# A two-part block on one core: mixers of the second part reordered, and the modulation ahead of the gathers moved off ScalarE

## The chip, the cores and the metric

One core of a Trainium2 chip runs the whole kernel. The metric is the device time of one execution in microseconds. The core has five engines with a queue each, worked off in order: TensorE (PE, matrix products into PSUM, and transposes), VectorE (DVE), ScalarE (ACT), GpSimd (POOL, which also issues the gathers) and SyncE (SP, which issues the weight loads). They wait for each other on semaphores only.

## The reference

One sequence of 256 tokens, width 1024, goes through two parts.

- First part: six modulation vectors `mod = silu(c) @ w_ada + b_ada` (each 1024 wide); an RMS norm with shift and scale; a projection; eight heads of forgetting attention and eight of stick-breaking attention, each head's output normed and all of them projected by `w_out`; then a second modulated norm and a layer that picks, for each token, 16 experts in each of 8 heads (128 rows of 2 x 1024 values per token, gathered from memory), takes 128 dot products, a gelu and a gated sum.
- Second part, two layers. Layer 0: a projection `x @ w_in`, rotary embedding, four heads of differential attention (two softmax maps a head, subtracted) with a norm, and four heads of plain causal attention ("moba", which is that at 256 tokens), both projected by `w_out`; a layer norm; a squared-relu feed-forward of width 4096; a layer norm. Layer 1: gated linear attention (GLA) with decays, a norm and a silu gate, then the same two norms and a feed-forward.

```python
mod = c_act @ w_ada[l] + b_ada[l]
a = diff_attention(dq, dk, dv, lam, subln, lambda_init)
b = moba_attention(mq, mk, mv)
return jnp.concatenate([merge_heads(a), merge_heads(b)], axis=-1) @ w_out
x = layer_norm(DEEPNORM_ALPHA * x + mix, ln_mix_g[l], ln_mix_b[l])
```

## The kernel before

**Weights.** Every weight matrix is cut in tiles of 1024 x 512 (2 MB). A tile is loaded whole in one of four buffers `W`; `load_on` (L347) issues the loads in the planned order, each once the tile before it in its buffer is done. A dense tile is then split in two parts of less precision, so that a product takes three matrix products: four pieces of `split_piece` (L359), each one ScalarE copy to `WH` (three buffers) and one subtraction to `WL` on VectorE. The splits do not stand where they are needed. They wait in a list `behind`; `tick(n)` (L366) takes up to n entries off its head while they may run (tile's load issued, the former tile in its `WH` buffer done), and `take` (L378) emits what is left of a tile just before its use. `fm_tile` (L524) runs a tile with features as rows (four half groups of 24 products with 256 columns, two to a PSUM bank); `tm_tile` (L539) runs it with tokens as rows (two groups of 24 products with 512 columns). Both call `tick` and a hook between groups, and the hook is how other work gets between dense products on TensorE's queue.

**Ahead of the gathers.** The modulation tiles 4 to 9 are made by `ada_rows` (L684). Of a tile's eight rows blocks VectorE multiplies and adds 0 to 3, ScalarE scales 4 to 7 (`some`, L692), and GpSimd adds up ScalarE's four results and VectorE's sum in four additions (`sums`, L706); both steps of a tile stand in `behind`. `close` (L715) is one product with ones on TensorE, which adds over the partitions. It ends the tile, so that the next load in its buffer starts. `stick_breaking` (L973) gives one step per hook: a score product, three ScalarE operations, two of VectorE and two of GpSimd for head i, a product and as many operations again for head i-1, and the values for head i-2. Order of the list: L811 to 816 and L983 to 1009.

**Gathers.** `gather` (L1352) issues 256 gathers from GpSimd, each 128 rows of 8 KB; VectorE takes the dot product, TensorE adds up. The last query tile (`queries`, L1297) is computed between the first four.

**Second part, layer 0.** After two V tiles come four projection tiles with rotary embedding (L1553 to 1556). `evac_rope` (L1526) copies a bank on ScalarE, has TensorE multiply the copy by a rotation matrix at once, and finishes on VectorE. Then `attention` (L822) runs twice as a generator, differential and moba attention in turn: each step emits the scores of head i (`scores`: per map one product pair, one VectorE pass, two maxima, two ScalarE exponentials), then the weights and transposes of head i-1 (`weights`, `turned`), then the values of head i-2. The norm of the differential output, the scaling of moba's and their transposes follow. `close_pair` (L551) runs the output projection and the layer norm.

**Layer 1.** `ffn` (L1648) ends in a layer norm whose second half of tokens is transposed at once (`give`, L477, `last`, L485). GLA: the narrow gate projection, q, the gate sums, k, two silu tiles, two V tiles; each group of these four calls the next step of `levels` (L1756: GpSimd makes decays, VectorE operands and results, TensorE products, eight levels). Then the head products, a norm per half of the tokens, the transposes, and `close_mixer` (L1689).

Of the kernel before, what the change touches and what calls it, by code (L numbers as in the profile page):

```python
# [182 lines left out]
def build(nc, A, out, C1, C2):  # L183
    ctx = ExitStack()
    with ctx:
# [48 lines left out]

        def bank():
            b = turn[0] % 4
            turn[0] += 1
            return b
# [53 lines left out]
        w_ada(9, 3)  # L292
        wout.append(wplan(A["w_out"], 0, 0, 0, 0))
        wq.append(wplan(A["w_query"], 0, 0, 2, 2))
        wout.append(wplan(A["w_out"], 0, 512, 3, 1))
# [6 lines left out]
        for j, s, h in ((2, 2, 0), (5, 1, 1), (0, 0, 2), (1, 3, 0), (3, 2, 1), (4, 1, 2)):  # L302
            hyt.append(wplan(A["hy_w_in_2"], 0, j * 512, s, h))
        later_w, later_h = itertools.cycle((0, 3, 2, 1)), itertools.cycle((0, 1, 2))
# [18 lines left out]
        gla_in = {j: wplan_on(A["gla_w_in_2"], 0, j) for j in (0, 1, 4, 5, 2, 3)}  # L323
# [200 lines left out]
        def fm_tile(tile, evac, *tokens, xtok=None, hook=None, n=2):  # L524

            take(tile)
            for c in range(0, 4, 2):
                b = bank()
                for j in range(2):
                    w = slice((c + j) * 128, (c + j + 1) * 128)  # L530
                    tk = dense(PS[b][:, j * 256:(j + 1) * 256], tile, fm_pairs(tile, w), *tokens, *bank_free[b], xtok=xtok)
                    if j == 1:
                        bank_free[b] = evac(b, c, tk)
                    tick(n)
                    if hook:
                        hook()
            wdone(tile, tk)

        def tm_tile(tile, evac, *tokens, hook=None, n=4):  # L539

            take(tile)
            for t in range(2):
                b = bank()
                tk = dense(PS[b][:, :], tile, tm_pairs(tile, t), *tokens, *bank_free[b], mid=hook)
                bank_free[b] = evac(b, t, tk)
                tick(n)
# [3 lines left out]

        def close_pair(pair, norm, *tokens, n=2):  # L551

            for t in range(2):
                for j in range(2):
                    b = bank()
                    take(pair[j])
                    tk = dense(PS[b][:, :], pair[j], tm_pairs(pair[j], t), *tokens, *bank_free[b], mid=norm.mid if (j, t) == (1, 1) else None)
                    if t == 1:
                        wdone(pair[j], tk)
                    norm.give(j, b, t, tk)  # L560
                    if (j, t) != (1, 1):
                        tick(n)
# [121 lines left out]
        def ada_rows(j, direct=()):  # L684
# [5 lines left out]
            t = {}  # L690

            def some(ks, kp):  # L692
                def step():
                    if ks[0] == 0:
                        accumulate(acc, tile, ks, *acc_free[half])
                    else:
                        for k in ks:
                            dve(lambda e: e.scalar_tensor_tensor(out=acc, in0=tile.w[:, k, :], scalar=silu_c[:, k:k + 1], in1=acc,
                                                                 op0=ALU.mult, op1=ALU.add))
                    t["d"] = dve.last  # L700
                    for k in kp:
                        t["a"] = act(lambda e: e.activation(tile.w[:, k, :], tile.w[:, k, :], ACT.Copy, scale=silu_c[:, k:k + 1]),
                                     t_cb, tile.arrived, ordered=False)
                return step

            def sums():  # L706
                w = tile.w
                pool(lambda e: e.tensor_tensor(w[:, 4, :], w[:, 4, :], w[:, 5, :], ALU.add), t["a"])
                if not direct:
                    pool(lambda e: e.tensor_tensor(w[:, 6, :], w[:, 6, :], w[:, 7, :], ALU.add))  # L710
                    pool(lambda e: e.tensor_tensor(w[:, 4, :], w[:, 4, :], w[:, 6, :], ALU.add))
                t["p"] = pool(lambda e: e.tensor_tensor(w[:, 4, :], w[:, 4, :], acc, ALU.add), t["d"])
                acc_free[half] = (t["p"],)

            def close():  # L715
                b = bank()
                tk = mm(PS[b][:, :], [(silu_c[:, k:k + 1].broadcast_to([128, 128]), tile.w[:, k, :]) for k in direct] +
                        [(ones, tile.w[:, 4, :])], t["p"], *bank_free[b])
# [8 lines left out]
            a, b = some((0, 1), (4, 5)), some((2, 3), () if direct else (6, 7))  # L727
            return [(cond, a), (cond, lambda: (b(), sums()))], (cond, close)
# [82 lines left out]
        later_split(win[1])  # L811
        t_zs = zero_q(QS, t_turned)
# [3 lines left out]
        later_ada(4)  # L816
# [156 lines left out]
        def stick_breaking():  # L973
            for i in range(10):
# [4 lines left out]
                if 0 <= i - 2 < 8:  # L979
# [3 lines left out]
        later_close(4)  # L983
# [4 lines left out]
        tm_tile(win[2], evac_tok(lambda t: V[:, t, 512:1024]), hook=lambda: hooks.pop(0)())  # L988
        t_vs = (act.last, dve.last)
        later_ada(5)  # L990
        later_ada(6)
        later_close(5)
# [5 lines left out]
        later_close(7)  # L998
# [5 lines left out]
                        values_in=lambda: t_vf)  # L1004
        later_ada(8)
        later_ada(9)
        later_close(8)
        later_close(9)
        later_split(wout[0])
# [4 lines left out]
        tm_tile(win[5], evac_tok(lambda t: V[:, t, 0:512]), hook=lambda: hooks.pop(0)(), n=5)  # L1014
# [3 lines left out]
        def norm_half(i, write):  # L1018
# [944 lines left out]
```

How the kernel before makes its waits and increments, by code:

```python
    def wait(self, *tokens):  # L100
        for sem, value in tokens:
            if value > self.seen.get(sem.name, 0):
                self.seen[sem.name] = value
                self.steps.append(lambda e, s=sem, v=value: e.wait_ge(s, v))
# [1 line left out]
    def __call__(self, make, *tokens, ordered=True):  # L106
        self.wait(*tokens)
        if ordered:
            self.wait(self.last)
        self.n += 1
        self.steps.append(lambda e, m=make(LATER), s=self.sem: m(e).then_inc(s, 1))
        return self.last
# [4 lines left out]
    def dma(self, make, slot, *tokens):  # L118
        self.wait(*tokens)
        slot.n += 16
        self.steps.append(lambda e, m=make(LATER), s=slot.sem: m(e).then_inc(s, 16))
        return (slot.sem, slot.n)
```

## Time and profile before

| | us |
|---|---|
| median of 3 runs | 1717.49 |
| lowest and highest run | 1708.98, 1719.38 |
| the profiled execution: whole time | 1713.44 |
| its span in the trace | 1711.6 |
| busy: TensorE, VectorE, ScalarE, GpSimd | 1380.6, 1131.3, 539.2, 454.7 |

Times in the trace are us from the start of the span. A row of a timeline or of the waits names what released the idle time before it; a line number can be that of a helper that records every operation, so the tile names say what the operation is: `W` a raw weight tile, `WH` and `WL` its split, `LNV<-W` the modulation's products, `EB<-PS` stick-breaking and the mixers' scores, `XH` and `XL` the split and transposed activations.

### The profile page before, as it was taken

How to read it: one execution, taken by the hardware profiler on the slowest of the kernel's cores; microseconds unless marked ns; L12 is line 12 of the kernel's file. 1: busy time of each engine (PE TensorE's matmuls, PEld its weight loads, DVE VectorE, ACT ScalarE, POOL GpSimd, SP SyncE). 2: the span in 40 equal slices, each digit the busy share in tenths (PEclk: the TensorE clock that was granted, in tenths of full speed). 3: DMA queues.
4: the chain of work that ended last, by engine and by line, in shares of the span. 5: the costliest groups of instructions: out<-in, count | busy, mean ns of one | idle time of the engine just before them, and what ended most of it. 6: DMA issues, size and time to landing. Idle time of an engine off the chain costs nothing.

```text
span 1711.6 us, 17345 instructions
## 1 busy us (share of the span) xinstructions
PE 1380.6 (81%) x6264; PEld 971.9 (57%) x6264; DVE 1131.3 (66%) x2051; ACT 539.2 (32%) x1023; POOL 454.7 (27%) x393
## 2 busy tenths in 40 slices
PE   6976788777777677777777788658999899789998
PEld 5875668523223232222222267547999687679996
DVE  6655665688887788886555556647756659577564
ACT  2453434222221213212111233323434246234341
POOL 1154305244443443544444200000211025001110
PEclk9988899999998999999999989878999999889999
DMA  9554526799999999999999823204555534245550
GB/s 367 190 184 148 196 74 227 293 421 409 421 421 412 421 408 382 400 422 420 422 421 421 344 75 123 98 25 142 182 196 197 189 110 147 75 151 179 188 197 25
DMA packets 116629, 433.17 MB, mean 253 GB/s; under 512 B 6832, under 2 KB 7088, under 8 KB 83520
## 3 DMA queue, kind: packets, MB, share of 16 engines
q0 software_dynamic: 36864, 268.45, 38.0%
q1 hardware_dynamic: 79392, 162.51, 26.8%
q8 instruction: 50, 0.82, 0.2%
q10 hardware_dynamic: 288, 1.11, 0.2%
q14 instruction: 35, 0.29, 0.0%
HBM read 431.00 MB, written 1.05 MB: 252 GB/s over the span
## 4 chain that ended last, share of the span: by engine, by line
PE 47%; DMA 23%; DVE 19%; ACT 6%; issue 2%; POOL 2%; SPq 0%; DVEq 0%; ACTq 0%; POOLq 0%
PE PS L45 45%; DMA EB<-in_experts,EI 22%; DVE EB L78 5%; DVE WL L75 3%; ACT BIG L24 2%; PE PS L84 1%; DVE X L63 1%; POOL W L75 1%; ACT WH L24 1%; DVE Y L75 1%; DMA W<-in_w_ada 1%; DVE GV L75 1%; DVE EB L63 1%; DVE XL L75 1%; DVE ST L69 1%
## 5 line engine op out<-in xcount | busy, mean ns | idle before, releaser
L45 PE MATMUL PS<-EB,BIG 128*128 128x512 f32 x1024 | 495.4, 628 | 169.9 <-ACT BIG L24 169.8
L45 PEld LDWEIGHTS PS<-EB,BIG 128*128 128x128 f32 x1024 | 190.3, 197 | 470.3 <-ACT BIG L24 287.3
L78 DVE CUSTOM_DVE_ANT_0 EB<-EB,Y 128x1024 f32<-128x1024 f32 x256 | 313.4, 1224 | 146.0 <-DMA EB<-in_experts,EI 145.0
L39 POOL DMA_INDIRECT EB<-in_experts,EI x256 | 288.3, 1126 | 397.0 <-PE PS L45 380.9
L75 DVE TENSOR_TENSOR WL<-W,WH 128x1024 fp32r<-128x1024 f32 x228 | 297.5, 1351 | 109.5 <-ACT WH L24 109.3
L45 PE MATMUL PS<-XH,WH 128*128 128x256 f32 x928 | 272.0, 293 | 12.8 <-DVE WL L75 10.0
L24 ACT ACTIVATE WH<-W 128x1024 fp32r<-128x1024 f32 x240 | 237.8, 1047 | 91.8 <-PE PS L45 84.9
L45 PE MATMUL PS<-XL,WH 128*128 128x256 f32 x928 | 265.0, 286 | 0.0
L45 PE MATMUL PS<-XH,WL 128*128 128x256 f32 x928 | 265.0, 286 | 0.0
L45 PEld LDWEIGHTS PS<-XH,WH 128*128 128x128 f32 x928 | 180.9, 195 | 17.9 <-DVE WL L75 11.1
L45 PEld LDWEIGHTS PS<-XL,WH 128*128 128x128 f32 x928 | 180.8, 195 | 2.7 <-issue 2.4
L45 PEld LDWEIGHTS PS<-XH,WL 128*128 128x128 f32 x928 | 180.6, 195 | 0.0
L24 ACT ACTIVATE BIG<-BIG 128x2 f32<-128x2 f32 (+1 forms) x136 | 31.1, 228 | 442.5 <-DVE BIG L78 442.0
L75 POOL TENSOR_TENSOR AL<-Y,AH 128x512 fp32r<-128x512 f32 x32 | 41.5, 1298 | 459.9 <-DVE AH L66 459.9
L24 ACT ACTIVATE BIG<-K,BIG 128x128 f32<-128x128 f32 x256 | 100.3, 393 | 58.8 <-DVE BIG L75 57.9
L45 PE MATMUL PS<-WH,XH 128*128 128x512 f32 x240 | 102.8, 428 | 10.8 <-DVE XL L75 6.4
L45 PE MATMUL PS<-WL,AH 128*128 128x512 f32 x256 | 101.3, 396 | 0.0
L45 PE MATMUL PS<-WH,AH 128*128 128x512 f32 x256 | 100.8, 394 | 0.0
L45 PE MATMUL PS<-WH,AL 128*128 128x512 f32 x256 | 100.3, 392 | 0.0
L45 PE MATMUL PS<-WL,XH 128*128 128x512 f32 x240 | 98.9, 412 | 0.0
L45 PE MATMUL PS<-WH,XL 128*128 128x512 f32 x240 | 98.7, 411 | 0.0
L24 ACT ACTIVATE Y<-Y 128x512 f32<-128x512 f32 (+1 forms) x40 | 28.7, 718 | 118.7 <-DVE Y L72 113.5
(170 smaller groups left out, 1512.1 us busy)
## 6 DMA issues: line engine op xcount, KB each, us to landing
W<-in_ffn_w SPq DMA_DIRECT2D x32, 2048.0 KB, 8.8
W<-in_w_ada SPq DMA_DIRECT2D x12, 2048.0 KB, 12.2
W<-in_w_in SPq DMA_DIRECT2D x6, 2048.0 KB, 12.9
W<-in_hy_w_in SPq DMA_DIRECT2D x6, 2048.0 KB, 13.5
W<-in_gla_w_in SPq DMA_DIRECT2D x6, 2048.0 KB, 7.9
W<-in_w_query SPq DMA_DIRECT2D x4, 2048.0 KB, 8.2
W<-in_w_out SPq DMA_DIRECT2D x2, 2048.0 KB, 8.3
EB<-in_experts,EI POOLq DMA_INDIRECT x256, 11.1
```

Source lines behind the costliest of these rows:

```text
L24: return lambda e: e.activation(*a, **k)
L39: return lambda e: e.indirect_dma_start(*a, **k)
L45: return lambda e: e.matmul(*a, **k)
L63: return lambda e: e.scalar_tensor_tensor(*a, **k)
L69: return lambda e: e.tensor_reduce(*a, **k)
L75: return lambda e: e.tensor_tensor(*a, **k)
L78: return lambda e: e.tensor_tensor_reduce(*a, **k)
L84: return lambda e: e.transpose(*a, **k)
```

## The change

Ahead of the gathers:
- `ada_rows` uses VectorE and GpSimd alone. VectorE takes row blocks 0 to 4, GpSimd multiplies 5, 6 and 7, and adds them and VectorE's sum: three steps in the list (products 0, 1 and GpSimd's 5; products 2, 3 and GpSimd's 6 with an addition; product 4 and GpSimd's 7 with two additions).
- The order in the list: tile 4's steps stand ahead of the first projection tile, tile 5's ahead of the third, each close one place earlier, and the split of `wout[0]` ahead of the last close. `tm_tile` gets ticks in the middle of a group (`inside`). `w_out`'s first tile is loaded ahead of modulation tile 9, in another buffer.
- `drain()` before the last query tile.

In the second part:
- `evac_rope` leaves the rotation for later; `behind_group`, the hook of the four tiles, runs it after the next half group. From the tenth of the 16 half groups on it also takes one step of the differential attention, so that its six steps stand among the last two tiles. Moba follows alone, with the norm of the differential output (`norm_half`) spread over its steps. The `WH` buffers of tile 6 of the projection and of the tiles behind it change, so that the mixers' buffers are free.
- The output projection first sums rows 0 to 511 (the differential half) of all four groups, with moba's scaling and transposes behind the first group, then rows 512 to 1023.
- `ffn(0)` leaves the transposes of its second half of tokens until two V groups of the GLA have run on the first half; the V tiles now stand ahead of the gate, q and k, and `levels` goes on in the middle of a group too, among the two silu tiles alone.
- The GLA's second half is normed before the output projection's first half runs, and transposed behind that.
- `bank()` no longer hands out a bank that is being filled.

```diff
-            a, b = some((0, 1), (4, 5)), some((2, 3), () if direct else (6, 7))
-            return [(cond, a), (cond, lambda: (b(), sums()))], (cond, close)
+            def products(ks):
+                for k in ks:
+                    if k == 0:
+                        accumulate(acc, tile, (0,), *acc_free[half])
+                    else:
+                        t["d"] = dve(lambda e: e.scalar_tensor_tensor(out=acc, in0=w[:, k, :], scalar=silu_c[:, k:k + 1], in1=acc,
+                                                                      op0=ALU.mult, op1=ALU.add))
+            def beside(k):
+                pool(lambda e: e.tensor_scalar(w[:, k, :], w[:, k, :], silu_c[:, k:k + 1], None, ALU.mult), t_cb, tile.arrived)
+                if k > 5:
+                    pool(lambda e: e.tensor_tensor(w[:, 5, :], w[:, 5, :], w[:, k, :], ALU.add))
+                if k == 7:
+                    t["p"] = pool(lambda e: e.tensor_tensor(w[:, 5, :], w[:, 5, :], acc, ALU.add), t["d"])
...
+            steps = [(cond, lambda ks=ks, k=k: (products(ks), beside(k))) for ks, k in (((0, 1), 5), ((2, 3), 6), ((4,), 7))]
...
         later_split(win[1])
+        later_ada(4)
...
-        later_close(4)
+        later_ada(5)
         later_split(win[3])
...
-        later_ada(5)
+        later_close(5)
         later_ada(6)
-        later_close(5)
         later_split(win[4])
...
+        def behind_group():
+            fresh[0] += 1
+            if fresh[0] % 2:
+                rotate_one()
+            if fresh[0] == 10:
+                mixing.append(attention(4, lambda i: QD[:, i, :], lambda i: KD[:, i // 2, :],
...
+                                        maps=2, lam=lam, tokens=(act.last, dve.last, *hyt[2].done), done=diff_done))
+            if fresh[0] >= 10:
+                next(mixing[0], None)
...
+        for _ in moba:
+            for _ in range(2):
+                if steps:
+                    steps.popleft()()
+            tick(2)
...
+                dense(PS[b][:, :], hy_out[j], tm_pairs(hy_out[j], t), diff_x["x", t], *bank_free[b], ks=range(4), stop=False)
+                if (j, t) == (0, 0):
+                    write_moba(0)
+                    write_moba(1)
+                else:
+                    tick(2)
...
+        ffn(0, t_xt, norm, beside=lambda free: wg_parts.append(narrow_parts(wg, 16, 0, t_wg, *free)), turn=False)
+        first_v = []
+        for j in range(2):
+            b = bank()
+            take(gla_in[2 + j])
+            first_v.append((b, dense(PS[b][:, :], gla_in[2 + j], tm_pairs(gla_in[2 + j], 0), norm.xt[0], *bank_free[b])))
+        norm.last()
...
         for j in range(2):
-            tm_tile(gla_in[4 + j], with_levels(evac_silu(j)), n=2)
-        for j in range(2):
-            tm_tile(gla_in[2 + j], with_levels(evac_tok(lambda t: VG[:, t, j * 512:(j + 1) * 512])), n=2)
+            tm_tile(gla_in[4 + j], with_levels(evac_silu(j)), hook=lambda: next(lv, None), n=2)
...
+        t_head_x = turn_tile(Y[:, 0, :], 0, gla_norm(0))
+        ready = gla_norm(1)
```

## Rows read from the trace of the kernel before

**Rows 1.** The chain that ended last, the page's shares by engine.

```profile
PE 47%; DMA 23%; DVE 19%; ACT 6%; issue 2%; POOL 2%; SPq 0%; DVEq 0%; ACTq 0%; POOLq 0%
```

**Rows 2.** Windows: stretch, length, PE, PEld, DVE, ACT, POOL busy, clock, DMA share, GB/s.

```profile
60.00:155.00 95.00, 79.01 (x492) 71.11 (x490) 53.86 (x67) 44.90 (x73) 42.59 (x50) 0.89 0.44 155
320.00:976.00 656.00, 485.87 (x1020) 187.94 (x1019) 476.76 (x1142) 140.46 (x414) 280.60 (x249) 0.97 1.01 415
1088.00:1129.00 41.00, 24.63 (x110) 21.55 (x111) 25.28 (x69) 13.67 (x52) 0.00 (x0) 0.72 0.08 32
1129.00:1147.00 18.00, 6.13 (x29) 4.50 (x28) 7.70 (x14) 6.42 (x12) 0.00 (x0) 0.59 0.00 0
1147.00:1182.00 35.00, 27.15 (x113) 21.55 (x113) 22.91 (x39) 8.76 (x15) 0.00 (x0) 0.84 0.43 150
1363.00:1399.00 36.00, 28.05 (x208) 26.92 (x209) 20.70 (x32) 15.90 (x21) 0.95 (x1) 0.86 0.38 128
1399.00:1470.00 71.00, 64.70 (x356) 54.38 (x355) 63.64 (x60) 33.30 (x40) 30.38 (x20) 0.99 0.42 148
1487.00:1523.00 36.00, 27.99 (x113) 22.23 (x114) 23.15 (x40) 9.40 (x16) 0.00 (x0) 0.83 0.48 162
```

**Rows 3.** Groups by form ahead of the gathers: count, busy, mean ns, idle before.

```profile
L75 POOL TENSOR_TENSOR W<-W 128x512 f32<-128x512 f32 x18 | 26.3, 1463 | 25.8 <-ACT W L24 24.5
...
L24 ACT ACTIVATE W<-W,ST 128x512 f32<-128x512 f32 x24 | 15.3, 706 | 0.0
```

**Rows 4.** Timeline of ScalarE: start, us, operation, idle before; stick-breaking, last evacuation.

```profile
90.18 0.49 ACT L24 ACTIVATE EB<-PS 128x384 f32<-128x384 f32 x1
...
96.73 0.49 ACT L24 ACTIVATE EB<-PS 128x384 f32<-128x384 f32 x1
...
154.03 0.60 ACT L24 ACTIVATE BIG<-PS 128x512 f32<-128x512 f32 x1 [5.96 <-PE PS L45]
```

**Rows 5.** Timeline of TensorE ahead of the gathers, two of its waits.

```profile
103.70 2.07 PE L45 MATMUL PS<-EB,K 128*128 128x256 f32 x6 [3.66 <-ACT W L24]
...
171.52 1.22 PE L45 MATMUL PS<-W,K 128*128 128x512 f32 x1 [8.85 <-POOL W L75]
```

**Rows 6.** Timeline of VectorE: one product alone, one beside GpSimd's additions.

```profile
131.49 0.75 DVE L63 SCALAR_TENSOR_TENSOR LNV<-W,ST,LNV 128x512 f32<-128x512 f32 x1
...
168.72 1.63 DVE L63 SCALAR_TENSOR_TENSOR LNV<-W,ST,LNV 128x512 f32<-128x512 f32 x1
```

**Rows 7.** Timeline, rotary projections: three rotation products, one VectorE operation behind them.

```profile
1031.15 2.08 PE L45 MATMUL PS<-BIG,GV 128*128 128x512 f32 x2 [3.23 <-ACT BIG L24]
...
1040.27 1.12 PE L45 MATMUL PS<-BIG,GV 128*128 128x512 f32 x2 [0.69 <-ACT BIG L24]
...
1047.68 1.13 PE L45 MATMUL PS<-BIG,GV 128*128 128x512 f32 x2 [0.69 <-ACT BIG L24]
...
1048.84 0.69 DVE L75 TENSOR_TENSOR Y<-PS,GV 128x512 f32<-128x512 f32 x1 [2.16 <-PE PS L45]
```

**Rows 8.** Timeline of VectorE in a mixer step: first score, first and last weights.

```profile
1102.86 0.56 DVE L63 SCALAR_TENSOR_TENSOR EB<-PS,K 128x384 f32<-128x384 f32 x1
...
1105.76 0.18 DVE L60 RECIPROCAL ST<-ST 128x4 f32<-128x4 f32 x1
...
1107.27 0.48 DVE L63 SCALAR_TENSOR_TENSOR EB<-EB,ST 128x256 f32<-128x256 f32 x1
```

**Rows 9.** Timeline of TensorE: waits behind the feed-forward's norm and the GLA's norm.

```profile
1369.54 1.97 PE L84 MATMUL PS<-K,X 128*128 128x128 f32 x8 [6.58 <-DVE X L63]
...
1483.60 2.15 PE L84 MATMUL PS<-K,Y 128*128 128x128 f32 x8 [5.03 <-DVE Y L63]
```

**Rows 10.** Groups by form: split halves at 60 to 245, and in the levels.

```profile
L75 DVE TENSOR_TENSOR WL<-W,WH 128x1024 fp32r<-128x1024 f32 x24 | 28.8, 1238 | 18.7 <-ACT WH L24 18.7
...
L24 ACT ACTIVATE WH<-W 128x1024 fp32r<-128x1024 f32 x28 | 28.0, 1045 | 2.2 <-DMA W<-in_w_in 2.1 <-issue 0.2
...
L75 DVE TENSOR_TENSOR WL<-W,WH 128x1024 fp32r<-128x1024 f32 x20 | 30.5, 1569 | 0.0
```

More of the change, by code:

```diff
@@ L689, in ada_rows @@
             o = GV[:, kind - 2, half * 512:half * 512 + 512]
[L690 to L695, printed above, removed]
-                    else:
[L697 to L713, printed above, removed]
+            w, t = tile.w, {}
@@ L1296, in build @@
         later_split(wq[3])
+        drain()
         queries = query_groups(3)
@@ L1564, in build @@
                          lambda h, t: V[:, t, 512 + h * 128:512 + (h + 1) * 128], 128, 6, 128.0 ** -0.5,
-                         part(GVf[:, 2688:3840], 3), [*part(BIG[:, 5120:5888], 2), buf(9)], tokens=t_proj, base=16, done=moba_done)
-        mixers = [diff, moba]
-        while mixers:
-            for g in list(mixers):
-                if next(g, True):
-                    mixers.remove(g)
-            tick(2)
-        hs, hr, ht = (a[:, 0:8] for a in (hs_, hr_, ht_))
-        tq = []
-        for t in range(2):
-            ta = act(lambda e: e.activation(Y[:, t, 0:512], PS[4 + t][:, :], ACT.Copy), diff_done["out"])
-            tq.append(act(lambda e: e.activation(PS[4 + t][:, :], Y[:, t, 0:512], ACT.Square), ta))
@@ L1890, in build @@
                     r.append(td)
-            t_heads.append(turn_tile(Y[:, t, :], t, r))
-        t_xt = t_heads[-2:]
+            return r
+        t_head_x = turn_tile(Y[:, 0, :], 0, gla_norm(0))
+        ready = gla_norm(1)
         ln_free[0] = (dve.last, pool.last, pe.last)
-        t_xt = close_mixer(1, gla_out, t_xt)
+        norm = layer_norm(A["ln_mix_g_2"][1], A["ln_mix_b_2"][1])
+        first = []
+        for j in range(2):
+            b = bank()
+            take(gla_out[j])
+            first.append((b, dense(PS[b][:, :], gla_out[j], tm_pairs(gla_out[j], 0), t_head_x, *bank_free[b])))
+        t_head_x = turn_tile(Y[:, 1, :], 1, ready)
+        for j, (b, tk) in enumerate(first):
+            norm.give(j, b, 0, tk)
+            tick(2)
+        for j in range(2):
+            b = bank()
+            tk = dense(PS[b][:, :], gla_out[j], tm_pairs(gla_out[j], 1), t_head_x, *bank_free[b], mid=norm.mid if j else None)
+            wdone(gla_out[j], tk)
+            norm.give(j, b, 1, tk)
+            if j == 0:
+                tick(2)
+        t_xt = norm.tokens
         t_out = []
```

190 lines of the change are left out of this document (110 added, 80 removed).

## The prediction

> **What bounds the kernel now.** I read the chain of work that ended last first: TensorE has 47% of it, transfers 23%, VectorE 19% [rows 1]. No engine bounds the whole, so the windows by stage come next [rows 2]. From 320 to 976 us the transfer engines are full (share 1.01, 415 GB/s); nothing in the change touches that stage, so it only moves as a block. All that can be won lies in stretches where TensorE is idle and its clock low: ahead of the gathers (79 of 95 us busy at a granted clock of 0.89), the mixers (24.6 of 41 at 0.72) and the norm behind them (6.1 of 18 at 0.59), and the joints around the feed-forwards. The levels of the GLA are the opposite: TensorE 64.7 and VectorE 63.6 of 71 us, both nearly full. The timelines then show each wait.
>
> **Ahead of the gathers.** Removed: 24 scalings on ScalarE, 15.3 us [rows 3]. Added: one VectorE product for each of six tiles, and two GpSimd operations for each (six for four). ScalarE's queue is where they hurt: at 103.70 TensorE waited 3.66 us with ScalarE's scaling ahead of the stick-breaking's exponential [rows 5].
> The sum goes by the pace of stick-breaking. A step without a wait took 96.73 - 90.18 = 6.55 us [rows 4]. Six more heads start, 39.3 us; the two last steps start none, and I take 9.7 for both (four half groups' pace below, less the missing score); two closes on the path are 0.9 each. 90.18 + 39.3 + 9.7 + 1.8 = 141.0, against the evacuation at 154.03 [rows 4]: at best 13 us. The loads allow it, since each close stands earlier: the tile that the last projection needs is freed one tile sooner. Against it stand GpSimd's operations. The second and third step come in one tick, five operations of 1.46 us [rows 3], 7.3 us, into a gap of some 5 between the mask operations of two heads; I charge 2.5 for each of the two tiles that lie beside stick-breaking, which leaves 8. The 8.85 us wait at 171.52 is that of tile 8's close for GpSimd [rows 5]. Its sums now begin a half group sooner, but VectorE's product and the last addition still follow the group: some 5 us stay, 3.9 go. Tile 9 is now loaded behind `wout[0]`, and its close stands in the forgetting attention: +3. Sum -9.
> GpSimd's multiplication by a column has no row. Nothing excludes that it is nearly free; above, its subtraction of twice the size is the next row, and the addition at 1.46 is nearest and is what I took. At 2.4 it costs three more per tile, of which about a third on the path: +6. Nearly free it gives -3. So this part is -20 (all waits gone) to +3.
> The other cost: VectorE's product takes 0.75 us alone and 1.63 beside GpSimd's additions [rows 6]. The Trainium skill (SBUF — State Buffer, "SBUF: two separate sides") has the access that the two share as an exclusive lock, held for a whole instruction, and the trace agrees. That rule speaks against moving ScalarE's part to GpSimd, and is the second rival below. The skill's GPSIMD Engine Reference (Engine selection) puts a one-input operation near line rate; by it a multiplication would be about half of the addition, some 0.7, this part -12 and the total 1687.5 as an estimate. No row here shows it.
> `drain()` I cost at nothing: VectorE and ScalarE reach those splits behind the same score evacuations as now.
>
> **Rotation.** TensorE waits for the ScalarE copy of each pair of half groups: 3.23 once and 0.69 seven times [rows 7]. Run a half group later, the copy is done: -8.1, call it -8. The cover is that half group: 7.41 us between two rotations (1040.27, 1047.68), less 0.69 and 1.12, is 5.6, so 2.8 each.
>
> **Mixers.** A differential step holds VectorE from 1102.86 to 1107.75, 4.9 us [rows 8], and TensorE's scores, transposes and values add 1.9: 6.8. A moba step by the same operations is 3.4. The sum, 10.2, is the pace of the present loop (41 us for four [rows 2]). TensorE runs in order, and the transposes of a step wait for weights that VectorE makes behind this step's scores. So a hook stops the dense products for its whole chain: putting the differential steps between half groups hides none of the 6.8. It exposes more. At group 10 the scores wait for the newest splits (copy 0.6, two of 1.05, one of 1.24 [rows 10]): 3.9. At 11 and 13 the rotation's three passes of 0.69 [rows 7] stand ahead, 1.5 each. At 14 the weights wait behind splits, 3.2. Sum 10.1; between 4 and 10.1 I take 8, as some splits will be early. Against it, the 18 us from 1129 to 1147 [rows 2] go: the differential norm lies in moba's steps, moba's scaling behind the first output group (2.8 us of cover for about 2). But in moba VectorE, the bound, gets that work and four pieces of split: 7.7 us and 5.0, with ScalarE's 4 x 1.05 in the same chain. Between 8 and 16 I take 10. 8 + 10 - 18 = 0. The clock: five half groups of 2.8 now stand among waits of 4 to 7 us, and such a stretch has 0.72 [rows 2]: 1.1 each, 5.4; it was granted 1.00 before. Half of it, +2.5, since the two last groups stand denser. The output projection keeps its order of size: its second halves leave less time (4.2 us) for the first norm (6), which eats what the earlier scaling gives. Sum +2.5, from -8 to +12.
>
> **Feed-forward to GLA.** The wait of 6.58 us [rows 9] disappears under two V groups, 11 us, and the clock stays up (0.86 in that stretch). But 22.2 us of dense products leave the levels, where they covered VectorE. What is late next: the dense work up to the first level ends at 1363 + 54 = 1417 (V 22.2, transposes 3.3, gate projection 2.8, q and k 22.2, the rest 3.6). VectorE's list in the levels is 63.6 less twelve pieces of 1.57 [rows 10] and two evacuations of 0.7: 43.4, and TensorE's 64.7 - 22.2 = 42.5, nearly equal, in turns; 5 us of mutual waits gives 1465.5 against 1469.5 now: -4, from -9 to +3.
>
> **GLA's output.** The projection starts on the first half while the second is normed: the 5.03 us [rows 9] go and TensorE starts 7 us sooner, then waits 2.4 for the second half's split: -4.5.
>
> **Sum.** -9 - 8 + 2.5 - 4 - 4.5 = -23, against the profiled execution's 1713.4 (span 1711.6): 1690.4, I say 1690.5. The median of the runs is 1717.5, 4 us above that execution, so this is 1.6% under it.
>
> **Rivals.**
> *More is hidden than I allow.* If stick-breaking meets its pace (-16), the mixers' splits are always early and the clock holds (-6), and the levels run without mutual waits (-9): -16 - 8 - 6 - 9 - 4.5 = -43.5, 1670. For it: the pace of 6.55 was really seen. Against: it asks for luck in three places.
> *The gain is given back to the shared engines.* All 30 products run at 1.63, 48.9 us, where 24 at the mean of the two rows, 1.19, are 28.6: +20 us on VectorE, and with 0.6 of it on the path, +12, the first part is +3. With the mixers at +5.5 and the levels at 0: +3 - 8 + 5.5 + 0 - 4.5 = -4, 1709.5. For it: the slower product [rows 6], and both engines full in the levels. Against: products have slack at 131, where one ran alone.
> *Slower.* The hooks keep TensorE's granted clock at its lower level, 1.2 GHz, from the ninth half group to the end of the output projection. The 22.2 us of projection double, the projection behind them goes from 27.2 at 0.84 to some 44 (+17), the mixers' 17.7 us at full clock to 35.5 (+11): +50, 1740. It decides once the mean clock there is under 0.55. Against: even the stretch that was idle for two thirds had 0.59 [rows 2].
>
> **Chances.** Forecast case 0.50 (1675 to 1706), more hidden 0.20, given back 0.20, slower 0.08, something else 0.02. The range 1664 to 1717 reaches into both neighbours and leaves 2 in 10 out. Under 1700.3 (1% below the median, about what a measurement of this kernel can tell from no change) lie the second case and four fifths of the first: 0.61; within 1%: 0.30; slower: 0.09.
>
> **What would show it.** Stick-breaking starts 6.5 to 7 us apart and the first gather some 9 us earlier; ScalarE without `W<-W`. No 0.69 waits before rotations. Hooks of 6.8 us among the last two projection tiles at a clock near 0.75, and moba with its norm in 25 to 29 us. No wait of 6.6 ahead of the GLA, but its levels ending only 4 us sooner. I am wrong if GpSimd's multiplication is far from the addition, if VectorE's products all take 1.6, or if a hook of the mixers costs much less or more than 6.8.

## The result and the profile after

The changed kernel takes 1744.25 us (median of 4 runs, 1743.53 to 1746.07) against 1715.83 of the kernel before: ratio 1.0175, 95% interval 1.0144 to 1.0207, which lies clear of no change. It is 28 us slower where I forecast 27 us faster, and outside my range. The profiled execution has a span of 1742.4 us.

The chain of work that ended last is shared out as before [rows 1]:

```profile
PE 47%; DMA 23%; DVE 20%; ACT 5%; issue 2%; POOL 2%; SPq 0%; DVEq 0%; ACTq 0%; POOLq 0%
```

Windows by stage of the changed kernel, with the columns of [rows 2]:

```profile
60.00:155.00 95.00, 76.67 (x487) 70.03 (x486) 57.95 (x68) 34.54 (x56) 57.35 (x57) 0.89 0.43 153
...
1060.00:1122.00 62.00, 38.87 (x220) 34.49 (x220) 29.68 (x64) 14.44 (x41) 0.00 (x0) 0.81 0.12 38
1122.00:1152.00 30.00, 14.20 (x56) 11.78 (x57) 18.81 (x36) 12.17 (x29) 0.00 (x0) 0.54 0.17 63
1152.00:1191.00 39.00, 28.93 (x126) 22.48 (x124) 23.03 (x40) 8.43 (x15) 0.00 (x0) 0.89 0.41 134
1363.00:1417.00 54.00, 50.99 (x289) 43.52 (x288) 36.65 (x52) 22.82 (x31) 0.96 (x1) 1.00 0.47 164
...
1445.00:1512.00 67.00, 42.10 (x204) 36.54 (x204) 39.93 (x47) 20.64 (x34) 18.36 (x13) 0.79 0.18 63
```

Ahead of the gathers ScalarE lost 10 us of work and GpSimd gained 15, and TensorE is no busier. From 1363 to 1417 TensorE works almost without a gap at full clock, as the new V groups were meant to bring; but behind 1445 it is busy 42 of 67 us, where the levels before had 64.7 of 71 [rows 2]. There the time went.

Five marks cut every trace into the same stages: the load of `hy_w_in` that the end of the last query tile releases (ahead of the gathers); the first product of the two V groups that stand ahead of the rotary projections (13.9 us of the stage are theirs); the first product of the layer 0 output projection; the first product of the feed-forward; the load of the second layer's `ln_ffn`, counted from that of the first.

| stage, us | before | after | difference | predicted |
|---|---|---|---|---|
| ahead of the gathers | 317.6 | 317.4 | -0.1 | -9 |
| gathers, to the V groups | 690.6 | 692.0 | +1.4 | 0 |
| rotary projection and mixers | 138.5 | 142.9 | +4.4 | -5.5 |
| output projection, layer 0 | 35.1 | 39.2 | +4.1 | 0 |
| `ln_ffn` to `ln_ffn` (feed-forward, GLA, its output) | 337.2 | 356.9 | +19.7 | -8.5 |
| span | 1711.6 | 1742.4 | +30.8 | -23 |

The rest of 1.3 us lies behind the last mark. The gathers' stage is the same code in all kernels of this study and lies between 686.4 and 692.0 us in their traces, so a difference of single traces under about 3 us says nothing there; the medians carry the verdicts.

### The profile page after: what moved, and what is told of

Its sections match the earlier page's. It is cut to its first block, busy times and chain, and to the rows that moved or that the text cites. A ratio compares the mean times of both kernels' runs of the same rounds, so it can differ in the third digit from the quotient of the medians.

```text
span 1742.4 us, 17343 instructions
## 1 busy us (share of the span) xinstructions
PE 1386.0 (80%) x6264; PEld 976.7 (56%) x6264; DVE 1144.5 (66%) x2058; ACT 523.7 (30%) x998; POOL 482.2 (28%) x405
## 4 chain that ended last, share of the span: by engine, by line
PE 47%; DMA 23%; DVE 20%; ACT 5%; issue 2%; POOL 2%; SPq 0%; DVEq 0%; ACTq 0%; POOLq 0%
PE PS L45 46%; DMA EB<-in_experts,EI 22%; DVE EB L78 4%; DVE WL L75 3%; ACT BIG L24 2%; DMA W<-in_w_ada 1%; PE PS L84 1%; DVE Y L75 1%; ACT WH L24 1%; DVE X L63 1%; DVE LNV L63 1%; DVE EB L63 1%; DVE ST L69 1%; DVE XL L75 1%; DVE GV L75 1%
## 5 line engine op out<-in xcount | busy, mean ns | idle before, releaser
L75 DVE TENSOR_TENSOR WL<-W,WH 128x1024 fp32r<-128x1024 f32 x228 | 305.2, 1387 | 131.6 <-ACT WH L24 131.5
```

The lines of the kernel that those rows point to most:

```text
L75: return lambda e: e.tensor_tensor(*a, **k)
```

## The experiments

Sixteen of the seventeen kernels are built on the kernel before, with parts of the change added. Each is timed against the kernel before on its own chip (medians 1714.35 to 1715.93).

**Each part alone.** The first four (`a_alone`, `rot_alone`, `mix_alone`, `gla_alone`) leave out the norm of the GLA and the transposes behind it, and the last three of them also carry one line of the part ahead of the gathers:

```diff
-        tm_tile(win[5], ..., hook=lambda: hooks.pop(0)(), n=5)
+        tm_tile(win[5], ..., hook=lambda: hooks.pop(0)(), n=3, inside=2)
```

> The kernel before with the part ahead of the gathers alone (modulation on VectorE and GpSimd, its order and its loads). Theory 1, the ledger of the two traces: each part does alone what its stretch shows in the changed kernel, and here that is 0 us (the last query tile ends at 317.58 before and 317.44 after), so the time is within 4 us of before and the wait at about 171 is 5 us. Theory 2, the parts disturb each other (loads and splits of one against another), and alone this part brings my -9: 0.995 of before.

> The kernel before with the rotation behind the next half group and nothing else changed. Both theories have the 0.69 us waits and the one of 3.23 us gone: -8 us, ratio 0.995. If the rotation's VectorE passes run into the first scores of the mixers instead, -5.

> The kernel before with the rotation deferred, the differential steps among the last projection tiles, the norm in moba's steps and the output projection in two halves of its sum. Theory 1: +8.6 us as in its stretch of the changed kernel, ratio 1.005, with TensorE waits of 4 to 6 us in five or six hooks. Theory 2: my -5.5, ratio 0.997. With rot_alone at -8, theory 1 puts +16 to +17 on the reordering itself.

> The kernel before with the V groups of the GLA ahead of gate, q and k, the transposes of the second half behind two of them, and the levels in the middle and at the end of the four silu groups. Theory 1: +19 to +20 us, ratio 1.011, with waits of 6 to 7 us for operands in the middle of each silu group. Theory 2: my -4, ratio 0.998.

Measured: 1707.23, 1686.93, 1707.05 and 1719.71 us (ratios 0.9951, 0.9840, 0.9966, 1.0036). None can be set against the kernel before as it stands. The next batch repeats the parts with the norm in place. `rot_tick` is `rot_alone` with the norm; the rotation and the line above are its only edits to the order of work:

```diff
+                turning.append(rotate)      # rotation product and its passes
...
+        fm_tile(hyt[2], evac_rope(...), *t_xt, hook=behind_group)   # and so hyt[3], hyt[4], hyt[5]
```

> The kernel before with the rotation deferred and with the last projection tile ahead of the gathers taking two entries of the list in the middle of a group and three behind it, in place of five behind it; nothing else. This is rot_alone with the GLA's norm, which rot_alone, mix_alone, a_alone and gla_alone leave out (in gla_alone in its new form, in the others in the old one), together with the same change of the list. Theory 1: the norm is worth 10 to 11 us by the load marks of the traces, so 1697 to 1698, ratio 0.990; the wait of 8.85 at 171 has become two waits of 2 and 4. Theory 2: the gain of rot_alone was the missing norm alone, and this is 1709, ratio 0.995.

> mix_alone with the GLA's norm in place and without the change of the list ahead of the gathers. Theory 1 (ledger of the traces, +8.6 us for rotation, mixers and output projection): 1719 to 1724, ratio 1.003 to 1.005. Theory 2 (my sum, -5.5): 1709, ratio 0.997.

> The kernel before with everything from the end of the first feed-forward to the second layer's output projection as in the changed kernel, the rest as before. Theory 1: +19 for the levels and -1 for the output, 1733, ratio 1.011. Theory 2 (my sum, -8.5): 0.995.

Measured: `rot_tick` 1699.35 us, ratio 0.9924 (0.9902 to 0.9946), so the missing norm is worth 12.4 us. `mix_only` 1727.0, ratio 1.0063 (1.0042 to 1.0084), 3 us above what its first theory had. `gla_only` 1732.72, ratio 1.0108 (1.0089 to 1.0126), as its first theory had it. Corrected by 12.4, `a_alone` is at 1719.6, 5 us above before. The correction is a rough one: it puts `gla_alone` at 1732.1, level with `gla_only`, although `gla_alone` has the middle tick too. By the marks:

| stage, us | before | rot_tick | mix_only | gla_only | after |
|---|---|---|---|---|---|
| ahead of the gathers | 317.6 | 314.4 | 321.1 | 318.4 | 317.4 |
| rotary projection and mixers | 138.5 | 128.1 | 142.9 | 139.1 | 142.9 |
| output projection | 35.1 | 35.1 | 39.1 | 34.9 | 39.2 |
| `ln_ffn` to `ln_ffn` | 337.2 | 337.2 | 338.9 | 360.7 | 356.9 |

Each part costs alone what its stage shows in the changed kernel; theory 2, a disturbance between parts, falls. The first row differs between kernels with the same code there (317.6, 321.1 and 318.4: mean 319.0), so I take means: the whole part ahead of the gathers (part A), in `a_alone`, the changed kernel and `lv_first` below (322.2, 317.4, 320.6), is 320.1, +1. The one line with the middle tick, in the eight kernels that otherwise have the old list and loads (309.7 to 315.2), is 313.3, nearly 6 us less than before. No run has this line alone.

**Levels.** `lv_first` changes the order of issue at the end of a silu group and nothing else:

```diff
                 tk = dense(PS[b][:, :], tile, tm_pairs(tile, t), *tokens, *bank_free[b], mid=mid)
+                if early:
+                    hook()
                 bank_free[b] = evac(b, t, tk)
...
-                if hook:
+                if hook and not early:
                     hook()
...
-            tm_tile(gla_in[4 + j], with_levels(evac_silu(j)), hook=lambda: next(lv, None), n=2)
+            tm_tile(gla_in[4 + j], with_levels(evac_silu(j)), hook=lambda: next(lv, None), n=2, early=True)
```

> The changed kernel, where at the end of each of the four silu groups the step of the levels is issued ahead of the group's evacuation and of the pieces of split, not behind them. Theory R (the ring: the operands that the next half group waits for stand behind the silu evacuation on ScalarE, VectorE and GpSimd and behind the splits): the three waits of 6.4 to 6.8 us fall to 2 to 3, and it is 10 to 13 us faster than the changed kernel, ratio to the kernel before 1.010. Theory W (too little dense work against VectorE's and GpSimd's own work in the levels, in whatever order): within 3 us of the changed kernel, ratio 1.016 to 1.018.

Measured: 1725.91 us, ratio 1.0068 (1.0046 to 1.0090), 18 us faster than the changed kernel; its last stage is 338.9 against 356.9. Here is the ring in the changed kernel, from the timelines of TensorE, ScalarE, VectorE and GpSimd in this order:

```profile
1446.29 3.78 PE L45 MATMUL PS<-Y 128*128 128x128 f32 x16 [6.36 <-DVE Y L75]
...
1465.35 3.78 PE L45 MATMUL PS<-GV 128*128 128x128 f32 x16 [6.84 <-DVE GV L75]
...
1453.96 0.60 ACT L24 ACTIVATE BIG<-PS 128x512 f32<-128x512 f32 x1 [5.51 <-PE PS L45]
1454.59 1.29 ACT L24 ACTIVATE BIG<-BIG 128x512 f32<-128x512 f32 x2
...
1462.09 1.06 ACT L24 ACTIVATE Y<-Y 128x1024 f32<-128x1024 f32 x1 [4.30 <-POOL Y L75]
...
1455.92 0.69 DVE L75 TENSOR_TENSOR BIG<-PS,BIG 128x512 f32<-128x512 f32 x1 [7.28 <-ACT BIG L24]
1456.87 4.18 DVE L75 TENSOR_TENSOR WL<-W,WH 128x1024 fp32r<-128x1024 f32 x2 [0.26 <-ACT WH L24]
1461.15 1.56 DVE L33 COPY_PREDICATED LNV<-GV,PS 128x512 f32<-128x512 int32 x2
1462.75 2.54 DVE L75 TENSOR_TENSOR GV<-BIG,GV 128x512 f32<-128x512 f32 x2
...
1456.69 1.30 POOL L75 TENSOR_TENSOR BIG<-BIG,LNV 128x512 f32<-128x512 f32 x1 [9.33 <-DVE BIG L75]
1458.43 6.31 POOL L75 TENSOR_TENSOR Y<-BIG 128x512 f32<-128x512 f32 x4 [0.44 <-POOL BIG L75]
```

A group ends and ScalarE evacuates it at 1453.96. VectorE's silu product follows at 1455.92, then its two pieces of split. GpSimd's silu product stands at 1456.69, and only behind it, from 1458.43 on, come the decays of two steps. Their exponential on ScalarE is at 1462.09, the operands on VectorE at 1462.75, and TensorE, which had only the first half of the next group to do (2.8 us), has waited since 1458.5 for them, until 1465.35. The next evacuation needs that group's second half. The ring turns once in 18.2 and 17.6 us (1453.96, 1472.12, 1489.68) for two steps. In the kernel before the products that need the operands stand a whole group later, and their waits are 0.28 to 1.0 us. With the step ahead of the evacuation the same two products wait less, and ScalarE's evacuations follow without a wait, 12.4 and 11.9 us apart:

```profile
1448.53 2.05 PE L45 MATMUL PS<-Y 128*128 128x128 f32 x16 [2.31 <-DVE Y L75]
...
1461.97 3.78 PE L45 MATMUL PS<-Y 128*128 128x128 f32 x16 [4.01 <-DVE Y L75]
...
1438.27 0.60 ACT L24 ACTIVATE BIG<-PS 128x512 f32<-128x512 f32 x1
...
1450.67 0.60 ACT L24 ACTIVATE BIG<-PS 128x512 f32<-128x512 f32 x1
...
1462.57 0.60 ACT L24 ACTIVATE BIG<-PS 128x512 f32<-128x512 f32 x1
```

Theory R holds, and by more than the 10 to 13 us that it said; theory W falls. From the second silu group to the head products TensorE waits 28.4 us in the changed kernel (6.36, 6.84, 6.71, 7.62, 0.91), 12.5 in `lv_first` (2.31, 4.01, 6.16) and 5.6 before (0.28, 0.71, 1.00, 3.61). What is left of the part was tried on top of `rot_tick` (the edit is that of `v_one` against `gla_combo`):

> rot_tick with the GLA of the changed kernel and the step of the levels ahead of each silu evacuation, as in lv_first. The parts add: gla_only gave +17.7 and lv_first took back 18, so 1699, ratio 0.992, level with rot_tick. Against it: if the parts of a kernel disturb each other by several us, it is 1705 or 1693.

> gla_combo with one V tile ahead of the levels and the other behind the silu tiles; one step of the levels at the end of each silu group (ahead of its evacuation), two in each of the last two V groups. The wait of 6.58 us at the end of the feed-forward stays filled by the one V group. If dense work between the steps is what was missing in gla_combo, the levels run at the old pace of 7 us a step and it is 4 to 7 us faster than rot_tick: 1693 to 1695, ratio 0.988. If two steps in a V group run into the same ring, level with rot_tick, 0.992.

```diff
-        for j in range(2):
+        for j in range(1):
...
-            tm_tile(gla_in[4 + j], with_levels(evac_silu(j)), hook=lambda: next(lv, None), n=2, early=True)
+            tm_tile(gla_in[4 + j], with_levels(evac_silu(j)), hook=ends_only, n=2, early=True)
+        tm_tile(gla_in[3], with_levels(evac_tok(...)), hook=lambda: next(lv, None), n=2, early=True)
```

Measured: `gla_combo` 1699.04 us, ratio 0.9917 (0.9888 to 0.9946); `v_one` 1699.46, ratio 0.9904 (0.9868 to 0.9940). Both are level with `rot_tick`, as the sum of the parts had it for the first, and the second does not bring the 4 to 7 us of its first theory. Their last stages are 337.9 and 337.2 against 337.2. The 6.58 us of the feed-forward [rows 9] are gone in each, and come back in the levels: in `v_one` TensorE is busy 29.8 of 43 us there and VectorE 36.5:

```profile
1417.00:1460.00 43.00, 29.75 (x160) 25.80 (x159) 36.50 (x38) 17.18 (x20) 16.25 (x11) 0.88 0.29 98
```

That VectorE's own list sets the pace once dense products leave is my reading of such windows; no run takes work off VectorE there, and it stays argued.

**Mixers.** `mix_late` starts the differential attention behind the last projection group; `mix_skew` keeps it in turn with moba, two steps ahead. Both have the middle tick of `rot_tick`, and the norm in moba's steps and the output projection of the changed kernel.

```diff
-            if fresh[0] == 10:
+            if fresh[0] == 16:
+                rotate_one()
...
-            if fresh[0] >= 10:
-                next(mixing[0], None)
```

> mix_only with the change of the list of rot_tick, and with the differential steps alone behind the last projection group, none among the groups. Theory H (steps among the half groups cost more than alone, by splits, rotation passes and the slower clock of the half groups; 42 us there): 6.8 us a step, 34 to 36 in all, so 7 us faster than mix_only with that list, 1715, ratio 1.000. Theory N (the order among the groups hides something; norm and output are the loss): 1723 to 1728, ratio 1.005 to 1.007.

> rot_tick with the differential attention two steps ahead of moba, the other four in turn with it as before, the differential norm in the last two steps of moba and the output projection in two halves of its sum. If the pairing in turn is what the changed kernel gave up (a pair takes 10.2 us, the two apart 6.8 and 7 to 8), the paired part costs as before, and the 18 us stretch of the norm shrinks by 8 while the two single steps and the output's second half take back 6 to 10: 1697 to 1701, ratio 0.991 to 0.993. If it is the norm's place that costs, 1708 or more, 0.996.

Measured: `mix_late` 1703.46 us, ratio 0.9926 (0.9901 to 0.9951); `mix_skew` 1704.56, ratio 0.9942 (0.9923 to 0.9961). Of the 23.5 us between `mix_only` and `mix_late`, 14.4 lie in the stage of the mixers (142.9 against 128.5) and 5.9 ahead of the gathers. Theory H holds, and by twice what I gave it; `mix_skew` lies between its two theories. Here are TensorE's waits in the changed kernel, with the steps among half groups (the first row is the first scores, the others are the weights), then those for the weights in `mix_late`, with the steps alone:

```profile
1059.96 2.90 PE L45 MATMUL PS<-BIG 128*128 128x128 f32 x8 [4.07 <-issue]
...
1073.97 0.90 PE L84 MATMUL PS<-K,EB 128*128 128x128 f32 x3 [5.92 <-DVE EB L63]
...
1084.29 0.90 PE L84 MATMUL PS<-K,EB 128*128 128x128 f32 x3 [4.34 <-DVE EB L63]
...
1097.62 0.90 PE L84 MATMUL PS<-K,EB 128*128 128x128 f32 x3 [5.84 <-DVE EB L63]
...
1109.13 0.90 PE L84 MATMUL PS<-K,EB 128*128 128x128 f32 x3 [6.05 <-DVE EB L63]
```

```profile
1081.35 0.90 PE L84 MATMUL PS<-K,EB 128*128 128x128 f32 x3 [4.43 <-DVE EB L63]
...
1088.52 0.90 PE L84 MATMUL PS<-K,EB 128*128 128x128 f32 x3 [3.71 <-DVE EB L63]
...
1096.98 0.90 PE L84 MATMUL PS<-K,EB 128*128 128x128 f32 x3 [3.71 <-DVE EB L63]
```

In `mix_late` the projection ends at the pace of `rot_tick` (70 us) and the differential attention takes 31.6 us behind it. In the changed kernel the two together take 112.3: 42 for the attention. The stage as a whole is 128.5 in `mix_late`, 128.2 in `mix_skew` and 128.1 in `rot_tick`: neither new order wins anything over the old loop with the norm behind it. No run keeps the old loop and moves the norm alone. And both pay for the output projection in two halves: 39.2 and 41.0 us against 35.1.

**Ahead of the gathers.** Five kernels, all with the rotation deferred and the middle tick in the last projection tile, separate the list, the loads and the engines:

> rot_tick with the whole new order ahead of the gathers (list, loads, ticks in the middle of a group, drain) but the modulation as before: four scalings on ScalarE, four additions on GpSimd a tile. Theory E (the move from ScalarE to GpSimd is what costs in this part, the order is free or brings a little): 1694 to 1700, at or below rot_tick, ratio 0.989 to 0.992. Theory O (the order and the later loads of the query tiles cost): 1704 to 1708, ratio 0.995.

> rot_tick with the modulation on VectorE and GpSimd as in the changed kernel (three steps a tile), in the old order of the list and with the old loads. Theory O (order_only has shown the loss of this part to be in the order, 7.7 us, and the move of the engines to be free there): 1697 to 1702, ratio 0.991 to 0.993. Theory E' (the move costs as much as the order, and the two only do not add because both hold the same GpSimd queue): 1705 to 1709, ratio 0.995.

> order_only with the loads as before (w_out's first tile behind modulation tile 9, in its old buffer). Theory L (the loads cost: the first query tile is loaded at 197 us in order_only and at 166 in rot_tick): as rot_tick, 1699 to 1702, ratio 0.992. Theory Q (the list costs: two tiles' additions stand ahead of stick-breaking's masks on GpSimd, waits of 7.03, 4.50 and 7.56 us): as order_only, 1705 to 1708, ratio 0.995.

> rot_tick with the loads of the changed kernel (w_out's first tile ahead of modulation tile 9 and in another buffer), the list and the engines as in rot_tick. Theory S (the gain of the new loads is theirs: list_only is at 1714.5 and order_only, which differs by the loads alone, at 1707.0): 1691 to 1693, ratio 0.987. Theory P (the loads pay only where the list holds the closes back): 1698 to 1703, ratio 0.992.

> loads_only with the middle tick in the third projection tile too (two entries in the middle of a group, two behind it, in place of four behind it). If what the middle tick buys in the last tile is the earlier close and nothing else, this does nothing here: within 2 us of loads_only. If GpSimd's additions come apart in general, 3 us faster.

| kernel | list | loads | scaling | stage, us | median, us | ratio (95%) |
|---|---|---|---|---|---|---|
| rot_tick | old | old | ScalarE | 314.4 | 1699.35 | 0.9924 (0.9902 to 0.9946) |
| loads_only | old | new | ScalarE | 317.0 | 1701.75 | 0.9929 (0.9903 to 0.9954) |
| loads_tick2 | old, one more middle tick | new | ScalarE | 314.0 | 1702.59 | 0.9944 (0.9922 to 0.9965) |
| list_only | new | old | ScalarE | 329.4 | 1714.49 | 1.0000 (0.9982 to 1.0018) |
| order_only | new | new | ScalarE | 320.5 | 1707.03 | 0.9950 (0.9934 to 0.9967) |
| eng_only | old | old | GpSimd | 328.2 | 1711.56 | 0.9974 (0.9956 to 0.9991) |

The new list costs 15 us with the old loads, twice what theory Q had, and the new loads give 7 of them back but nothing by themselves (theory P). The move from ScalarE to GpSimd costs 12 us in the old order (theory E', and more than it said; `eng_only` also has three entries a tile in the list for two); in the new order it costs nothing that can be seen (320.5 against the mean of 320.1 with all of part A). The cause that theories Q and E' give, GpSimd's queue in front of stick-breaking's masks, is there. GpSimd and TensorE in `list_only`:

```profile
83.19 5.80 POOL L75 TENSOR_TENSOR W<-W 128x512 f32<-128x512 f32 x3 [15.75 <-ACT W L24]
89.14 2.06 POOL L75 TENSOR_TENSOR W<-W,LNV 128x512 f32<-128x512 f32 x1
...
94.67 2.08 PE L45 MATMUL PS<-EB,K 128*128 128x256 f32 x6 [7.15 <-POOL EB L75]
```

Tile 5's additions come 14 us sooner than in the kernel before (96.71), and the first mask of stick-breaking stands behind them. But this is not where the 15 us go:

| time in the trace, us | before | rot_tick | order_only | list_only | eng_only | after |
|---|---|---|---|---|---|---|
| last wait for a mask ends | 144.3 | 144.4 | 143.7 | 145.5 | 152.5 | 146.5 |
| last product of the last projection tile | 182.9 | 181.5 | 180.5 | 182.6 | 181.9 | 179.7 |
| first transposes behind the forgetting attention | 210.9 | 206.8 | 212.9 | 221.9 | 221.5 | 211.8 |

At the end of the last projection tile `list_only` and `eng_only` are at most 1 us behind `rot_tick`; the forgetting attention behind it takes 39.3 and 39.6 us where it took 25.3. ScalarE and then TensorE in `list_only`, and the same in `eng_only`:

```profile
208.38 1.06 ACT L24 ACTIVATE WH<-W 128x1024 fp32r<-128x1024 f32 x1 [9.98 <-DMA W<-in_w_out]
...
210.36 0.90 PE L84 MATMUL PS<-K,EB 128*128 128x128 f32 x3 [4.74 <-ACT EB L24]
...
191.14 1.06 ACT L24 ACTIVATE WH<-W 128x1024 fp32r<-128x1024 f32 x1 [7.17 <-DMA W<-in_w_out]
...
196.28 0.90 PE L84 MATMUL PS<-K,EB 128*128 128x128 f32 x3 [7.68 <-ACT EB L24]
```

ScalarE stands at the split of a `w_out` tile that is still being loaded (in `list_only` its load is issued at 200.18, behind the close of tile 9 at 198.13), and the exponentials that TensorE waits for stand behind that split. `rot_tick` has 1.28 us of this wait, and the kernel before, `order_only` and the changed kernel have none there: with the new loads the `w_out` tiles are issued 11 to 14 us apart at 157.1 and 171.0 (`order_only`) or 158.0 and 169.3 (changed). This fits that the new loads help the new list only, and that the move to GpSimd costs with the old loads only. It is read from the traces; no run moves these splits alone. The 7 us by which the forgetting attention of `order_only` (32.4) is still longer than that of `rot_tick` (25.3) have another cause, which stays open.

The middle tick works ahead of that. In the kernel before GpSimd's sums of tiles 8 and 9 were issued one behind the other at 165.11 and 171.61, and TensorE stood 8.85 us at the first of their closes [rows 5]. In `rot_tick` they start at 158.20 and 168.72 (TensorE's closes, then GpSimd):

```profile
164.81 1.12 PE L45 MATMUL PS<-W,K 128*128 128x512 f32 x2 [2.06 <-POOL W L75]
...
174.49 2.08 PE L45 MATMUL PS<-W,K 128*128 128x512 f32 x2 [3.91 <-POOL W L75]
...
158.20 4.67 POOL L75 TENSOR_TENSOR W<-W 128x512 f32<-128x512 f32 x3 [8.93 <-ACT W L24]
```

A second middle tick, in the third tile, does nothing (1702.59 against 1701.75), as it should if the tick works through that close. The best kernels are `rot_tick`, `gla_combo` and `v_one`, which cannot be told apart: 1699 us, 0.8 to 1% under the kernel before and 2.6% under the changed one. `rot_tick` has the shortest edit.

## Why the prediction was wrong, point by point

**Ahead of the gathers: -9 forecast, 0 in the pair of traces, +1 over all.** The failed step is the pace of stick-breaking, with the 2.5 us charged for each lump of GpSimd's operations. The pace was to be 6.55 us; eight heads started between 84.11 and 136.31, 7.5 apart, against 7.6 before (85.77 to 139.26). By the end of the last projection tile the sum had 12 us less (8 by the pace, 3.9 at the wait at 171); it is 3.3 less (179.7 against 182.9). The forgetting attention behind it, with +3 for tile 9's close, takes 32.1 us against 28.0. The wait of 3.66 for ScalarE went, and GpSimd took its place. TensorE's waits and GpSimd's groups in the changed kernel:

```profile
92.09 2.08 PE L45 MATMUL PS<-EB,K 128*128 128x256 f32 x6 [4.59 <-POOL EB L75]
...
116.08 2.07 PE L45 MATMUL PS<-EB,K 128*128 128x256 f32 x6 [4.97 <-POOL EB L75]
...
146.47 2.07 PE L45 MATMUL PS<-EB,K 128*128 128x256 f32 x6 [5.84 <-POOL EB L75]
...
167.18 2.07 PE L45 MATMUL PS<-W,K 128*128 128x512 f32 x2 [4.72 <-POOL W L75]
```

```profile
L72 POOL TENSOR_SCALAR W<-W,ST 128x512 f32<-128x512 f32 x15 | 28.5, 1898 | 17.2 <-DMA W<-in_w_ada 15.7 <-POOL EB L75 0.5
...
L75 POOL TENSOR_TENSOR W<-W 128x512 f32<-128x512 f32 x11 | 15.1, 1377 | 0.9
```

The three waits ahead of stick-breaking's second product are 15.4 us together; before, its own were 3.66 and 3.10 and a split's was 3.45, 10.2. The multiplication that I took at 1.46 takes 1.90: a third above the price taken, inside my bounds. The wait at 171, forecast at 5, is 4.72: that term was right. The middle tick, which the sum has in the 3.9 at that wait, is worth nearly 6 us by the means above; the list spent it. The rule of my sum that each close frees its tile sooner failed too: the load of the last projection's tile is issued at 129.43 against 130.14.

**Rotation: -8 forecast, -10.4.** The step held (128.1 against 138.5), but not quite as priced. TensorE's waits for ScalarE's copies fell from 8.0 us (eight) to 1.1 (two, of 0.39 and 0.69; the last rotation still follows its copy at once), 6.9 for the 8.1 forecast. The rest came with the clock, which the sum left out. The four projection tiles before, and in `rot_tick`, with 401 products each:

```profile
1022.10:1088.20 66.10, 55.86 (x401) 49.45 (x399) 42.67 (x52) 20.13 (x25) 1.89 (x2) 0.97 0.44 151
...
1015.40:1071.40 56.00, 52.71 (x401) 48.10 (x399) 43.14 (x52) 20.16 (x25) 1.90 (x2) 1.00 0.51 179
```

**Mixers and output projection: +2.5 forecast, +18.9.** By terms: the hooks cost 42.5 us among the groups against 31.6 alone (`mix_late`), 10.9, where I had 8 and 2.5 for the clock; the first scores wait 4.07 for 3.9 forecast. That step was right, in mechanism and size. The failed step is "8 + 10 - 18 = 0" in its last two terms. The 41 us of the old loop were split into four differential steps of 6.8, 27.2, and the rest for moba, and 18 us of norm were to become 10 in moba's steps: a gain of 8. But six differential steps run, and alone they take 31.6, which is 4.4 more; and moba with its norm takes 27.0 in `mix_late` for 23.8, which is 3.2 more (my signs, with 25 to 29, did not fit my own sum). Together they eat the gain: the stage is 128.5 against 128.1. In the changed kernel the stretch from the last step among the groups to the first output product takes 30.7 us; there moba's scores also wait 2.24 for the last rotation, which in `mix_late` lies ahead of the differential attention. That the two attentions in turn had hidden each other's chains is argued and not shown: `mix_skew` keeps them in turn for four steps and is no faster.

Output projection: 0 forecast, +4.1. Most of it is moba's transposes, which now stand in this stage: TensorE waits 2.14 us for the second four of them (1157.99), and they take 0.60 and 0.66. The cover that the second halves leave is a small part: the waits for the norm are 1.10 and 5.83 us, against one of 6.44 before.

**Feed-forward to GLA: -4 forecast, +22.** (294.7 and 316.8 us, from the load of `ln_ffn` to the first transposes of the GLA's output.) The wait of 6.58 went and the clock came up, as forecast; the failed step is "5 us of mutual waits", where the levels wait for 28.4. I added up lists of VectorE and TensorE and did not follow one operand through the queues. The mid-group hook needs what the hook before it issued only half a group earlier, behind the whole silu evacuation; `lv_first` prices that at 18 us. The rest of the way to the forecast stays open: with the steps ahead of the evacuation the last stage is 338.9 us, against 337.2 before and a forecast of 8.5 less.

**GLA's output: -4.5 forecast, -2.5.** (45.2 and 42.7 us, from those transposes to the feed-forward's first product.) The wait of 5.03 went, and the one of 2.4 that I put in its place is there, 2.46 at 1527.29. But TensorE then waits 7.57 us for the norm's second half at 1548.71, 6.43 at that place before. That is 1.1 of the 2 us missing; no run separates the rest.

**The rivals.** "Given back to the shared engines" had the mean product at 1.63; the 22 that one group of the changed kernel holds took 1.01 each, those before 1.07, so its mechanism fell. Its +3 for the first part is near the measured 0 to +1 by luck: TensorE waits for GpSimd's queue there, not for VectorE's products. A slowdown of VectorE there was, but in the splits (last section). "Slower", at 1740, names a time near the measured one by a mechanism that is not there: the clock was 0.81 from 1060 to 1122, 0.54 in the 30 us behind and 0.89 in the output projection, 0.78 over the whole, against its bound of 0.55, and the larger loss lies in the GLA, which it did not name.

## What to carry to other kernels

A hook in the middle of a dense group is only worth what stands between it and the hook that made its operands: follow one operand through each in-order queue, with the evacuation and the splits issued in between, before adding up busy times. Issue the next step's producers ahead of a group's evacuation, not behind it. When work moves to an engine that already holds small operations on the path, price what queues in front of those, not the work itself. An in-order queue also waits for transfers: a split of a tile that is still on its way held ScalarE for 10.0 and 7.2 us with the exponentials behind it, so a list of work has to be checked against the loads. And try every line of a large change alone, since a change of one tick count was worth 6 us that the rest of its part gave away.

## What the hardware showed that I had not expected

GpSimd's multiplication of 128x512 f32 by a column takes 1.90 us on average (15 in the changed kernel) and 1.97 in `eng_only` (18), single ones from 1.56 to 3.47, where its addition of two such tensors takes 1.38 and 1.40, the quickest 1.27. The one-input operation is the slower one. The Trainium skill (GPSIMD Engine Reference, Engine selection) has one-input operations near line rate; the trace disagrees, and the measurement decides.

VectorE's products did not slow with GpSimd busy 57 of 95 us in place of 43: 1.01 us each. Its subtractions of the splits did. The 24 between 60 and 245 us took 28.8 us before, 1.24 each and none over 1.48 [rows 10], and in the changed kernel

```profile
L75 DVE TENSOR_TENSOR WL<-W,WH 128x1024 fp32r<-128x1024 f32 x24 | 34.4, 1472 | 15.9 <-ACT WH L24 15.9
```

with single ones of 2.33. Three of them that ran from 83.79 took 5.01 us while GpSimd multiplied and added (83.42 to 87.72). `rot_tick` has 1.24, `eng_only` (old list, scaling on GpSimd) 1.38 and `list_only` (new list, scaling on ScalarE) the same 1.47. So either change is enough, and it is not the move to GpSimd as such; what counts, as I read it, is what GpSimd does during the splits.
